# Forgetful attention: cumulative gates as a 65th row of the keys, and the first projections of one token block placed during the other block's norm

## The chip, the core and the metric

The kernel runs on one core of a Trainium2 chip. Its time is the device time of one execution in microseconds (us). Engines are named as the profile names them: PE is TensorE's matmuls and PEld its weight loads, DVE is VectorE, ACT is ScalarE, POOL is GpSimd, SP is the sync engine, which here only issues DMAs. "The granted clock" is the share of TensorE's full speed that the throttle lets through: 1.00 is 2.4 GHz and 0.50 is 1.2 GHz.

## What is computed

The kernel computes two models one after the other on 256 tokens of width 1024: a first one (a chunk mixer, a state space mixer, and two layers that gather experts from a table, "peer"), and a second one (this attention, a conv feed-forward block, a latent attention, another feed-forward block). The change touches the attention of the second model, `fox_mixer`, and the place where the first model hands over to it:

```python
def fox_mixer(h, w_in, b_f, w_out):                      # 16 heads of 64
    proj = h @ w_in                                      # queries, keys, values, 16 gate columns
    logf = log_sigmoid(proj[..., 3 * FOX_WIDTH:] + b_f)
    cum = cumsum(logf, axis=1)                           # over the 256 tokens
    ...
    sc = einsum('bqhd,bkhd->bhqk', qi, k) * scale        # per block of 128 queries
    sc = sc + (cum_q[..., :, None] - cum_k[..., None, :])
    sc = where(kpos <= qpos, sc, -inf)
    p = softmax(sc)
    return einsum('bhqk,bkhd->bqhd', p, v) ... @ w_out
```

Everything here is float32. Its input `h` is the first model's result after two RMS norms in a row (`final_g`, then `fox_norm`).

## The kernel before

Each engine has its own program, and they meet only at semaphores. `first_pe`, `first_act`, `first_dve`, `first_pool` and `first_sync` are the first model's programs, and `pe_`, `act_`, `dve_` and `sync` inside `fox` (L2586 to L2863) are the attention's. The order on an engine is the order in which the code is written.

**The hand-over.** The last part of the first model is `peer1`, which goes through expert rows: POOL gathers them, DVE takes dot products with the tokens (L1496), ACT makes weights (L1377 to L1382), and PE adds the weighted rows up (L1308). The tokens are two blocks of 128 (tb 0 and tb 1). When block 0's last sum is added to XA, `Ends` (L1526 to L1585) norms it twice (ACT L1553 squares and L1556 square roots, DVE L1575 scales), transposes it on PE (L1584), and ACT copies it to HT (L1561), all among `peer1`'s last rows. Block 1 can be normed only once `peer1` has ended: DVE L1471 and L1473 add its last sums, then the same chain runs with nothing beside it.

**The attention's start.** PE waits until both blocks are in HT. Then it forms the gate sums (L2706: the 128 tokens of a block are the weights, 16 gate columns are streamed), and `project(0, 0)`: queries and keys of two heads (L2642, all 256 tokens streamed past 128 weight columns) and values of four heads (L2651). DVE and ACT turn the gate sums into log-sigmoids LF (L2800 to L2805, with Exp and Ln on ACT).

**Pairs.** The 16 heads are done as 8 pairs, two pairs (s = 0 and 1) to a round r. For a pair PE does `scores`, then the next projection (L2642 after s = 0; L2642 and L2651 after s = 1), then `values`: six transposes of the softmax numerators (L2680) and the products with the values (L2688 to L2690). `scores` forms, for each head, a product of queries and keys over 64 rows (L2663, L2667), and adds the gates' part as a matmul too: LT is the triangle matrix times the head's column of LF, made by DVE for each pair (`gates`, L2768), and is multiplied with the matrix SUF (L2665, L2669, L2670), so that a sum over tokens between key and query comes out. Scores are formed in pieces of 128 by 128 (first query block) and 128 by 256 (second). DVE adds the causal mask (L2776), takes row maxima (L2781, L2783), ACT takes exponentials (L2733). ACT also saves what the projection left in PSUM: queries L2719, keys L2720, values L2723, and then the transposed numerators for `values` (L2740). ACT's order in a round is: exponentials, saves of the projection, copies L2740.

**Weights.** SP issues three 1 MB loads per round (L193), each into a slot that it takes when `w_used` says that the slot's last projection has ended.

After the last pair the outputs are transposed (L339) and multiplied with `fox_out` (L390).

## Time and profile before

| | us |
|---|---|
| median of 3 runs | 3567.14 (3567.11 to 3570.8) |
| the profiled execution, its own time | 3568.08 |
| its span, first to last instruction | 3566.1 |
| `peer1`'s last sums on PE end | 2701.4 |
| first scores of the attention (L2663) | 2737.9 |
| last scores of the attention end, transposes of its outputs (L339) begin | 2856.1, 2865.0 |

A row of the timeline has its start in us from the span's start, the time from the first to the last of the merged instructions, the engine, the line of the code, the operation with output and inputs, and their number; in brackets the time that the engine stood idle before it, and what ended that. One float32 matmul of the code appears in the trace as two PE instructions, each with its own weight load, so 16 matmuls are x32. Merged matmuls overlap at their ends; what counts is the distance from the start of one to the start of the next.

### The profile page before, as it was taken

The page shows a single profiled execution, that of the slowest core. Times are in us where ns is not written, and L with a number is a line of the kernel's source. Part 1 is how long each engine was busy: PE and PEld are TensorE (multiplying, and loading weights), DVE is VectorE, ACT ScalarE, POOL GpSimd, SP SyncE. Part 2 cuts the span into 40 slices and gives each one's busy share as a digit, 9 for nine tenths or more (in the row PEclk, how much of TensorE's full clock was granted, in tenths as well). Part 3 has the DMA queues.
Part 4 walks back from the last instruction along what each step waited for, and adds up shares of the span by engine and source line. Part 5 has one row for each costly group of instructions (what it writes and reads, how often), then busy time and mean ns, then how long its engine had stood idle before and what let it go on. Part 6 is the DMA issues. An engine that isn't in the chain of part 4 may idle for free.

```text
span 3566.1 us, 53144 instructions
## 1 busy us (share of the span) xinstructions
PE 2822.0 (79%) x19152; PEld 1680.4 (47%) x19152; DVE 2225.3 (62%) x5084; ACT 1393.8 (39%) x3587; POOL 854.8 (24%) x780
## 2 busy tenths in 40 slices
PE   4988898777776877786575977777767989999998
PEld 3877344233222433341144722222115879877997
DVE  5855766768777666678735467777763246523276
ACT  1213444434433334443334243334433247523275
POOL 0001433334343333433400133344440000000000
PEclk8988999999888998886677999999768999999999
DMA  8888999999999999999967699999994235433353
GB/s 328 309 313 347 419 420 420 420 420 408 421 420 394 420 414 415 413 412 387 361 224 257 256 421 421 421 414 421 416 413 159 112 124 194 156 118 109 118 192 127
DMA packets 177293, 1153.12 MB, mean 323 GB/s; under 512 B 21892, under 2 KB 30492, under 8 KB 43436
## 3 DMA queue, kind: packets, MB, share of 16 engines
q0 software_dynamic: 111632, 810.60, 55.4%
q1 hardware_dynamic: 59244, 321.94, 24.1%
q10 hardware_dynamic: 6192, 17.67, 1.3%
q8 instruction: 130, 2.13, 0.2%
q14 instruction: 95, 0.78, 0.1%
HBM read 1128.86 MB, written 21.27 MB: 323 GB/s over the span
## 4 chain that ended last, share of the span: by engine, by line
PE 40%; DMA 37%; DVE 11%; issue 6%; ACT 5%; POOL 1%; SPq 1%; ACTq 0%; DVEq 0%; POOLq 0%
DMA AR<-in_peer_uv,AR 32%; PE PS L2829 10%; PE PS L1308 6%; DVE AR L1496 4%; DMA W<-in_ada_w 3%; PE PS L1266 2%; PE PS L660 2%; PE PS L3327 2%; DVE AR L1471 2%; PE PS L2642 2%; PE PS L390 2%; PE PS L2060 2%; POOL AR L1520 1%; PE PS L521 1%; PE PS L1924 1%
## 5 line engine op out<-in xcount | busy, mean ns | idle before, releaser
L1308 PE MATMUL PS<-AR 64*64 64x512 f32 x6144 | 984.3, 720 | 498.7 <-ACT AR L1382 497.3
L1496 DVE CUSTOM_DVE_ANT_0 AR<-AR,H 128x1024 f32<-128x1024 f32 x768 | 938.4, 1224 | 540.8 <-DMA AR<-in_peer_uv,AR 534.6
L1520 POOL DMA_INDIRECT AR<-in_peer_uv,AR x768 | 850.1, 1107 | 1615.1 <-PE PS L1308 1156.8
L1308 PEld LDWEIGHTS PS<-AR 64*64 64x64 f32 x6144 | 180.1, 148 | 945.3 <-ACT AR L1382 830.0
L1377 ACT ACTIVATE SM<-SM 128x1 f32<-128x1 f32 x768 | 155.5, 202 | 1171.1 <-DVE SM L1496 1170.3
L1266 PE MATMUL PS<-HT,W 128*128 128x256 f32 x1280 | 427.8, 440 | 0.0
L1266 PEld LDWEIGHTS PS<-HT,W 128*128 128x128 f32 x1280 | 217.4, 200 | 424.7 <-issue 413.0
L1382 ACT ACTIVATE AR<-AR,SM 128x64 f32<-128x64 f32 x768 | 267.2, 348 | 25.2
L2829 PE MATMUL PS<-XP,WP 128*128 128x256 f32 x2112 | 258.4, 284 | 6.4 <-ACT AR L3003 3.5
L2829 PEld LDWEIGHTS PS<-XP,WP 128*128 128x128 f32 x2112 | 257.3, 193 | 8.7 <-DVE WP L3026 3.8
L1379 ACT ACTIVATE SM<-SM 128x1 f32<-128x1 f32 x768 | 226.3, 295 | 25.0
L660 PE MATMUL PS<-W,HT 128*128 128x256 f32 x768 | 199.4, 400 | 16.5 <-ACT AR L725 13.2
L3026 DVE TENSOR_TENSOR WP<-W,WP 128x2048 fp32r<-128x2048 f32 x62 | 141.8, 2287 | 100.3 <-ACT WP L2989 100.3
L660 PEld LDWEIGHTS PS<-W,HT 128*128 128x128 f32 x768 | 149.2, 199 | 58.9 <-issue 37.3
L1471 DVE TENSOR_TENSOR AR<-PS,AR 64x512 f32<-64x512 f32 x192 | 132.2, 689 | 5.7 <-PE PS L1308 2.2
L2829 PE MATMUL PS<-WP,GVP 128*128 128x512 f32 x528 | 129.2, 402 | 7.4 <-DVE GVP L2824 7.4
L2989 ACT CAST WP<-W 128x2048 fp32r<-128x2048 f32 x62 | 118.8, 1916 | 0.0
L2829 PEld LDWEIGHTS PS<-WP,GVP 128*128 128x128 f32 x528 | 101.5, 195 | 28.9 <-issue 8.2
L521 PE MATMUL PS<-W,SM 128*2 128x64 f32 x3072 | 65.8, 254 | 60.0 <-DMA W<-in_ada_w 56.8
L521 PEld LDWEIGHTS PS<-W,SM 128*2 128x2 f32 x3072 | 56.2, 99 | 70.7 <-DMA W<-in_ada_w 51.6
L3327 PE MATMUL PS<-HT,W 128*128 128x256 f32 x288 | 63.2, 380 | 0.8 <-ACT HT L3201 0.8
L1377 ACT ACT_TABLE_LOAD x49 | 62.9, 1283 | 0.9
(402 smaller groups left out, 3394.7 us busy)
## 6 DMA issues: line engine op xcount, KB each, us to landing
W<-in_ada_w SPq DMA_DIRECT2D x48, 1024.0 KB, 8.0
W<-in_peer_w_q SPq DMA_DIRECT2D x44, 1024.0 KB, 9.5
W<-in_ffn_out SPq DMA_DIRECT2D x22, 1024.0 KB, 4.8
W<-in_ffn_gate SPq DMA_DIRECT2D x20, 1024.0 KB, 4.8
W<-in_ffn_val SPq DMA_DIRECT2D x20, 1024.0 KB
W<-in_cm_w_in SPq DMA_DIRECT2D x16, 1024.0 KB, 8.4
AR<-min_scr SPq DMA_DIRECT2D x16, 1024.0 KB, 6.7
AR<-in_peer_uv,AR POOLq DMA_INDIRECT x768, 15.7
```

The source lines that it names most:

```text
L521: mm = pe.matmul(PS[32 * c:32 * c + 2, self.bank, j * ADA_PART:(j + 1) * ADA_PART], CS[:, k, :], W[:, s, at:at + ADA_PART], start=(k == 0) ...
L660: mm = pe.matmul(self.bank(i)[:, j * COLS:(j + 1) * COLS], HT[:, k, tb * P:(tb + 1) * P], W[:, slot, k * COLS:(k + 1) * COLS], start=(k == ...
L1266: mm = pe.matmul(PS[:, j % 2, 0:2 * P], weights[:, k * COLS + (j % 2) * P:k * COLS + (j % 2 + 1) * P], HT[:, k, first:first + 2 * P], star ...
L1308: mm = pe.matmul(PS[c * self.HP:(c + 1) * self.HP, 4 + (u % 2) * 2 + half, :], self.DIAG[rows_, r % 4, :], self.UV[rows_, r % RING, D + c ...
L1377: a.activation(self.GELU[:, u % 2, one], self.ACTV[:, u % 2, one], ACT.Gelu_apprx_tanh).then_inc(gelu_done.sem, 1)
L1379: a.mul(self.WGT[:, u % 2, one], self.GELU[:, u % 2, one], self.GATE[:, u % 2, one]).then_inc(w_ready.sem, 1)
L1382: a.mul(self.DIAG[:, r % 4, :], self.EYES, self.WGT[:, u % 2, k:k + 1]).then_inc(diag_ready.sem, 1)
L1471: one = v.tensor_tensor(self.YG[out, cols], PS[here, 4 + (u % 2) * 2 + i, :], gate[here, cols], ALU.mult)
L1496: v.tensor_tensor_reduce(rows_, rows_, H[:, self.tb(u), :], 1.0, 0.0, ALU.mult, ALU.add, self.ACTV[:, u % 2, k:k + 1]).then_inc(u_used.sem, 1)
L1520: g.indirect_dma_start(out=self.UV[:, r % RING, :], out_offset=None, in_=t["peer_uv"], in_offset=bass.IndirectOffsetOnAxis(ap=self.IDS[:, ...
L2829: mm = pe.matmul(out, lhs[i], rhs[j], start=(start and n == 0), stop=(stop and n == 2))
L3026: v.tensor_tensor(parts[:, 1, :], block_of(s, c), parts[:, 0, :], ALU.subtract).then_inc(split_done, 1)
```

## The change

- The weight columns of queries and keys are stored in another order: each 128 columns are now one head's 64 query columns and its 64 key columns, where they were 128 query columns of two heads, then their 128 key columns. A projection has the same matmuls as before. ACT's two saves take 64 partitions of 512 elements instead of 128 of 256, and keys go to KP, which now keeps all 16 heads.
- Row 65 (index 64) of KP holds minus the cumulative gates of each key, and row 65 of QP ones, so the key's part of the gates comes out of the same matmul as the product (65 rows). LT, SUF, DVE's `gates` and their matmuls go. The query's part is added by DVE with the mask, in one instruction for each piece (four in place of two).
- The cumulative gates are made once: `cumulate` does six small matmuls, ACT copies one result (16 by 256, with scale -1), SP stores it as row 65 of KP by a DMA of 16 KB, DVE copies the other result for the queries.
- Gate sums and the first projection are done token block by token block. Block 0's part (`first_rows`) is placed in PE's program before the transposes of block 1. Block 1's part stands where all of it stood.
- ACT gets a square root of one element before block 1's norms. The load of SUF goes.

```diff
@@ first_pe, first_act
             peer1.pe(ends.pe(0), lambda: drain(norm2d.pe((1,))))
+            first_chunk["fox_rows"]()
             drain(ends.pe(1))
...
             peer1.act(ends.act(0), lambda: drain(norm2d.turned((1,))))
+            a.activation(SM[:, 503:504], IDENT[:, 0:1], ACT.Sqrt)
             drain(ends.act(1))
@@ fox
-            QP, KP = view(4096, 2, SEQ), view(4608, 2, SEQ)
-            LT = view(5120, 2, SCORES)
+            QP = view(4096, 4, SEQ)
+            CUM, CI, CIJ = view(5120, SEQ), view(5376, 2, FOX_H), view(5408, 2, 2)
+            KP = view(18432, FOX_H, SEQ)
-            SUF = view(27552, 2, SEQ)
+            ONE = FOX_D + 1
@@ fox: parameters, sync
-                sp.dma_start(SUF.rearrange("p b k -> p (b k)"), t["consts"][:, C_SUF:C_SUF + 2 * SEQ]).then_inc(par_in, 16)
...
-                with sp.Fori(0, ROUNDS) as r:
+                load(0, uw[0], t["fox_qk"][0])
+                load(2, uw[2], t["fox_v"][0])
+                load(1, uw[1], t["fox_qk"][1])
+                sp.wait_ge(f_fn, 3)
+                sp.dma_start(KP[FOX_D:ONE, :, :], CUM[0:FOX_H, :]).then_inc(par_in, 16)
+                with sp.Fori(1, ROUNDS) as r:
@@ fox: new functions
+            def first_gates(tb):
+                for k in range(KT):
+                    mm = pe.matmul(PS[:, 3, tb * FOX_H:(tb + 1) * FOX_H], HT[:, k, tb * P:(tb + 1) * P], FW[:, k, :],
+                                   start=(k == 0), stop=(k == KT - 1))
+                if tb:
+                    mm.then_inc(f_sums, 1)
+
+            def first_queries(tb):
+                pe.wait_ge(w_full[0], (uw[0] + 1) * 16)
+                for i in range(2):
+                    for k in range(KT):
+                        mm = pe.matmul(PS[:, 0, i * SEQ + tb * P:i * SEQ + (tb + 1) * P], W[:, 0, k * COLS + i * P:k * COLS + (i + 1) * P],
+                                       HT[:, k, tb * P:(tb + 1) * P], start=(k == 0), stop=(k == KT - 1))
+                if tb:
+                    mm.then_inc(w_used[0], 1)
+
+            def first_values(tb):
+                pe.wait_ge(w_full[2], (uw[2] + 1) * 16)
+                for k in range(KT):
+                    mm = pe.matmul(PS[:, 2, tb * COLS:(tb + 1) * COLS], HT[:, k, tb * P:(tb + 1) * P],
+                                   W[:, 2, k * COLS:(k + 1) * COLS], start=(k == 0), stop=(k == KT - 1))
+                if tb:
+                    mm.then_inc(w_used[2], 1)
+
+            def cumulate():
+                pe.wait_ge(f_arg, 3)
+                for half, parts in enumerate((((0, 0),), ((0, P), (1, SEQ)))):
+                    for n, (tb, at) in enumerate(parts):
+                        pe.matmul(PS[0:FOX_H, 5, half * P:(half + 1) * P], LF[:, tb, :], TRI[:, at:at + P],
+                                  start=(n == 0), stop=(n == len(parts) - 1))
+                for half, parts in enumerate((((0, 0),), ((0, P), (1, SEQ)))):
+                    for n, (tb, at) in enumerate(parts):
+                        mm = pe.matmul(PS[:, 6, half * FOX_H:(half + 1) * FOX_H], TRI[:, at:at + P], LF[:, tb, :],
+                                       start=(n == 0), stop=(n == len(parts) - 1))
+                mm.then_inc(f_sums, 1)
+
+            def first_rows():
+                pe.wait_ge(n_ht.sem, ht_at - 2)
+                pe.wait_ge(par_in, 32)
+                pe.wait_ge(sums_taken.sem, st)
+                first_gates(0)
+                first_queries(0)
+                first_values(0)
@@ fox: scores
-                    pe.wait_ge(lt_ready, j * 2 + 2)
                     pe.wait_ge(s_taken, 1 + j * 2)
-                    for i, h in enumerate(heads):
-                        pe.matmul(PS[:, 3 + i, 0:P], QP[h, s, 0:P], KP[h, s, 0:P], start=True, stop=False)
-                    for i in range(2):
-                        pe.matmul(PS[:, 3 + i, 0:P], LT[:, i, 0:P], SUF[:, 0, 0:P], start=False, stop=True)
-                    for i, h in enumerate(heads):
-                        pe.matmul(PS[:, 3 + i, P:SCORES], QP[h, s, P:SEQ], KP[h, s, :], start=True, stop=False)
-                    for i in range(2):
-                        pe.matmul(PS[:, 3 + i, P:SCORES], LT[:, i, P:SEQ], SUF[:, 0, :], start=False, stop=False)
-                        mm = pe.matmul(PS[:, 3 + i, P:SCORES], LT[:, i, SEQ:SCORES], SUF[:, 1, :], start=False, stop=True)
+                    for lo, hi, keys in ((0, P, P), (P, SCORES, SEQ)):
+                        for i in range(2):
+                            mm = pe.matmul(PS[:, 3 + i, lo:hi], QP[0:ONE, 2 * s + i, lo:lo + P],
+                                           KP[0:ONE, ds(r * 4 + (2 * s + i), 1), 0:keys], start=True, stop=True)
@@ fox: start of pe_
                 pe.wait_ge(n_ht.sem, ht_at)
+                first_gates(1)
+                first_queries(1)
+                cumulate()
+                first_values(1)
                 pe.wait_ge(par_in, 48)
-                pe.wait_ge(sums_taken.sem, st)
-                for tb in range(2):
-                    for k in range(KT):
-                        mm = pe.matmul(PS[:, 7, tb * FOX_H:(tb + 1) * FOX_H], HT[:, k, tb * P:(tb + 1) * P], FW[:, k, :],
-                                       start=(k == 0), stop=(k == KT - 1))
-                mm.then_inc(f_sums, 1)
-                project(0, 0)
@@ fox: act_
-                    a.activation(QP[:, s, :], PS[:, s, 0:SEQ], ACT.Copy, scale=FOX_D ** -0.5).then_inc(qk_saved, 1)
-                    a.copy(KP[:, s, :], PS[:, s, SEQ:2 * SEQ]).then_inc(qk_saved, 1)
+                    a.activation(QP[0:FOX_D, 2 * s:2 * s + 2, :], PS[0:FOX_D, s, :].rearrange("p (h t) -> p h t", h=2),
+                                 ACT.Copy, scale=FOX_D ** -0.5).then_inc(qk_saved, 1)
+                    a.copy(KP[0:FOX_D, ds(r * 4 + 2 * s, 2), :], PS[FOX_D:P, s, :].rearrange("p (h t) -> p h t", h=2)).then_inc(qk_saved, 1)
...
-                save(0, 0)
+                save_heads(0, 0)
+                a.wait_ge(f_sums, 2)
+                a.activation(CUM[0:FOX_H, :], PS[0:FOX_H, 5, 0:SEQ], ACT.Copy, scale=-1.0).then_inc(f_fn, 1)
+                save_values(0)
@@ fox: dve_
-                def gates(j):
-                    v.wait_ge(att_sums, j)
-                    for i in range(2):
-                        for lo, hi, tb in ((0, SEQ, 0), (SEQ, SCORES, 1)):
-                            one = v.tensor_tensor(LT[:, i, lo:hi], TRI[:, lo:hi], LF[:, tb, ds(j * 2 + i, 1)].to_broadcast([P, hi - lo]), ALU.mult)
-                        one.then_inc(lt_ready, 1)
+                def query_cums(j):
+                    dve.link(v, v.tensor_copy(CIJ, CI[:, :, ds(j * 2, 2)]))
...
-                        last = v.tensor_tensor(SB[:, i, :], PS[:, 3 + i, 0:SCORES], FOX_MASK, ALU.add)
+                        for q, (lo, hi) in enumerate(PIECES):
+                            last = v.scalar_tensor_tensor(SB[:, i, lo:hi], PS[:, 3 + i, lo:hi], CIJ[:, q, i:i + 1], FOX_MASK[:, lo:hi], ALU.add, ALU.add)
...
+                dve.link(v, v.memset(QP[FOX_D:ONE, :, :], 1.0))
...
+                v.wait_ge(f_sums, 2)
+                dve.link(v, v.tensor_copy(CI, PS[:, 6, 0:2 * FOX_H].rearrange("p (t h) -> p t h", t=2)))
@@ host side: order of the weight columns (one head's 64 query columns, then its 64 key columns ...)
-        "fox_qk": blocks(np.concatenate([q, k], -1).reshape(D, -1)), "fox_v": blocks(v.reshape(D, -1)),
+        "fox_qk": blocks(np.stack([x.reshape(D, FOX_H, FOX_D) for x in (q, k)], 2).reshape(D, -1)), "fox_v": blocks(v.reshape(D, -1)),
```

On PE, at the hand-over from `peer1` to the attention, before (L1584 is the transposing of a token block, L2706 the gate sums, L2642 and L2651 the projection, L2663 the first scores; here a float32 matmul is one):

```order
L1308 MATMUL PS<-AR 64x512 x12
L1584 MATMUL PS<-CON,H 128x128 x8
L2706 MATMUL PS<-AR,HT 128x16 x16
L2642 MATMUL PS<-HT,W 128x256 x16
L2651 MATMUL PS<-W,HT 128x256 x16
```

and after (L1582 is the transposing, L2640, L2649 and L2657 are `first_gates`, `first_queries`, `first_values`, L2666 and L2670 `cumulate`):

```order
L1306 MATMUL PS<-AR 64x512 x12
L2640 MATMUL PS<-AR,HT 128x16 x8
L2649 MATMUL PS<-HT,W 128x128 x16
L2657 MATMUL PS<-W,HT 128x256 x8
L1582 MATMUL PS<-CON,H 128x128 x8
L2640 MATMUL PS<-AR,HT 128x16 x8
L2649 MATMUL PS<-HT,W 128x128 x16
L2666 MATMUL PS<-CON,AR 16x128 x3
L2670 MATMUL PS<-AR,CON 128x16 x3
L2657 MATMUL PS<-W,HT 128x256 x8
```

Half of the gate sums and of the projection now stand ahead of block 1's transposes, and the query matmuls are twice as many with half as many columns each.

On PE, the scores of a pair with the projection behind them, before:

```order
L2663 MATMUL PS<-AR 128x128 x2
L2665 MATMUL PS<-AR 128x128 x2
L2667 MATMUL PS<-AR 128x256 x2
L2669 MATMUL PS<-AR 128x256
L2670 MATMUL PS<-AR 128x256
L2669 MATMUL PS<-AR 128x256
L2670 MATMUL PS<-AR 128x256
L2637 ISA
L2639 ISA
L2642 MATMUL PS<-HT,W 128x256 x16
```

and after:

```order
L2712 ISA
L2712 MATMUL PS<-AR 128x128
L2712 ISA
L2712 MATMUL PS<-AR 128x128
L2712 MATMUL PS<-AR 128x256 x2
L2687 ISA
L2689 ISA
L2692 MATMUL PS<-HT,W 128x256 x16
```

Ten matmuls have become four, of the same shapes.

On ACT, at the same hand-over and the attention's start, before (L1553 and L1556 are the norms of block 1, L1561 the copy of its transposes):

```order
L1382 ACTIVATE AR<-AR,SM 128x64
L1553 ACTIVATE AR,SM<-XA 128x1024
L1556 ACT_TABLE_LOAD
L1556 ACTIVATE SM<-SM 128x1
L1553 ACTIVATE AR,SM<-XA 128x1024
L1556 ACTIVATE SM<-SM 128x1
L1561 COPY HT<-PS 128x4x128 x2
```

and after (two lines of the code earlier, L1551 to L1559; L2490 is the added square root):

```order
L2490 ACT_TABLE_LOAD
L2490 ACTIVATE SM<-CON 128x1
L1551 ACTIVATE AR,SM<-XA 128x1024
L1554 ACTIVATE SM<-SM 128x1
L1551 ACTIVATE AR,SM<-XA 128x1024
L1554 ACTIVATE SM<-SM 128x1
L1559 COPY HT<-PS 128x4x128 x2
```

The table load of the square root stands ahead of the first squares instead of behind them.

## Rows read from the trace of the kernel before

**Rows 1.** Windows of one core, all engines: busy us and count, granted clock, DMA.

```profile
core 0: us, PE busy (x) PEld busy (x) DVE busy (x) ACT busy (x) POOL busy (x), PEclk, DMA share, GB/s
2700.00:2722.00 22.00, 9.39 (x46) 8.11 (x46) 7.25 (x12) 6.68 (x11) 0.00 (x0) 0.61 0.37 144
2740.00:2850.00 110.00, 105.84 (x560) 90.58 (x559) 30.60 (x108) 27.33 (x87) 0.00 (x0) 1.00 0.28 104
```

**Rows 2.** TensorE's timeline: start us, us, engine, line, output<-inputs, count, idle before.

```profile
2700.29 1.09 PE L1308 MATMUL PS<-AR 64*64 64x512 f32 x8 [0.58 <-ACT AR L1382]
2713.02 1.97 PE L1584 MATMUL PS<-CON,H 128*128 128x128 f32 x8 [11.64 <-DVE H L1575]
2715.66 7.01 PE L2706 MATMUL PS<-AR,HT 128*128 128x16 f32 x32 [0.68 <-ACT HT L1561]
2722.51 8.55 PE L2642 MATMUL PS<-HT,W 128*128 128x256 f32 x32
2737.90 0.49 PE L2663 MATMUL PS<-AR 64*128 64x128 f32 x4
2738.97 0.70 PE L2667 MATMUL PS<-AR 64*128 64x256 f32 x4
2739.60 0.70 PE L2669 MATMUL PS<-AR 128*128 128x256 f32 x2
...
2741.43 7.07 PE L2642 MATMUL PS<-HT,W 128*128 128x256 f32 x32
...
2749.82 0.43 PE L2688 MATMUL PS<-AR 128*128 x2 [0.67 <-ACT AR L2740]
```

**Rows 3.** VectorE's timeline before and after the gap.

```profile
2711.68 1.29 DVE L1575 SCALAR_TENSOR_TENSOR H<-XA,SM,AR 128x1024 f32<-128x1024 f32 x1
...
2725.03 0.19 DVE L2805 SCALAR_TENSOR_TENSOR AR<-AR 128x32 f32<-128x32 f32 x1 [1.36 <-ACT AR L2754]
...
2742.09 1.02 DVE L2776 TENSOR_TENSOR AR<-PS,CON 128x384 f32<-128x384 f32 x2 [15.66 <-PE PS L2670]
```

**Rows 4.** ScalarE's timeline of the same stretch.

```profile
2706.83 1.28 ACT L1556 ACT_TABLE_LOAD   x1
...
2738.01 0.58 ACT L2723 COPY AR<-PS 128x512 f32<-128x512 f32 x1 [6.26 <-PE PS L2651]
...
2748.53 0.38 ACT L2719 ACTIVATE AR<-PS 128x256 f32<-128x256 f32 x1 [0.80 <-PE PS L2642]
2749.07 0.88 ACT L2740 COPY AR<-PS 128x384 f32<-128x384 f32 x2
```

**Rows 5.** The sync engine's timeline: issues of the first two weights.

```profile
2699.69 0.36 SPq L193 DMA_DIRECT2D W<-in_fox_qk  x1
2700.34 0.33 SPq L193 DMA_DIRECT2D W<-in_fox_v  x1
```

**Rows 6.** DMA issues: KB each, median us to landing; the first two are those of rows 5.

```profile
W<-in_fox_qk SPq DMA_DIRECT2D x1, 1024.0 KB, 4.9
W<-in_fox_v SPq DMA_DIRECT2D x1, 1024.0 KB, 6.7
AR<-in_ffn_conv SPq DMA_DIRECT2D x2, 88.0 KB, 1.9
lag_scr<-H ACTq DMA_DIRECT2D x48, 16.0 KB, 3.9
```

**Rows 7.** TensorE's timeline elsewhere: matmuls with 128 columns at the full clock.

```profile
1999.35 7.41 PE L1236 MATMUL PS<-HT,W 128*128 128x128 f32 x64 [0.73 <-ACT HT L584]
```

**Rows 8.** Windows around the gap and the end of the stage.

```profile
2716.00:2722.00 6.00, 6.00 (x30) 6.00 (x29) 0.00 (x0) 0.91 (x1) 0.00 (x0) 0.50 0.00 0
2859.00:2868.00 9.00, 7.37 (x32) 6.66 (x33) 1.04 (x5) 3.71 (x12) 0.00 (x0) 0.50 0.13 54
```

**Rows 9.** TensorE's timeline at the stage's end.

```profile
2849.58 0.82 PE L2680 MATMUL PS<-CON,AR 128*128 128x128 f32 x6
...
2859.60 1.78 PE L2680 MATMUL PS<-CON,AR 128*128 128x128 f32 x6 [3.50 <-ACT AR L2733]
```

More of the change, by code:

```diff
@@ L62 @@
 C_ALL = 1808
-C_SUF = C_ALL
 class Signal:
@@ L2632, in sync @@
                 out_sync()
+            def first_gates(tb):
[37 more added lines that the diff above has]
+                first_values(0)
+            first_chunk["fox_rows"] = first_rows
             def pe_():
@@ L2657, in scores @@
                     pe.wait_ge(qk_saved, j * 2 + 6)
-                    pe.wait_ge(lt_ready, j * 2 + 2)
                     pe.wait_ge(s_taken, 1 + j * 2)
-                    heads = [slice(i * FOX_D, (i + 1) * FOX_D) for i in range(2)]
-                    for i, h in enumerate(heads):
-                        pe.matmul(PS[:, 3 + i, 0:P], QP[h, s, 0:P], KP[h, s, 0:P], start=True, stop=False)
-                    for i in range(2):
-                        pe.matmul(PS[:, 3 + i, 0:P], LT[:, i, 0:P], SUF[:, 0, 0:P], start=False, stop=True)
-                    for i, h in enumerate(heads):
-                        pe.matmul(PS[:, 3 + i, P:SCORES], QP[h, s, P:SEQ], KP[h, s, :], start=True, stop=False)
-                    for i in range(2):
-                        pe.matmul(PS[:, 3 + i, P:SCORES], LT[:, i, P:SEQ], SUF[:, 0, :], start=False, stop=False)
-                        mm = pe.matmul(PS[:, 3 + i, P:SCORES], LT[:, i, SEQ:SCORES], SUF[:, 1, :], start=False, stop=True)
+                    for lo, hi, keys in ((0, P, P), (P, SCORES, SEQ)):
+                        for i in range(2):
+                            mm = pe.matmul(PS[:, 3 + i, lo:hi], QP[0:ONE, 2 * s + i, lo:lo + P],
+                                           KP[0:ONE, ds(r * 4 + (2 * s + i), 1), 0:keys], start=True, stop=True)
                     mm.then_inc(att_sums, 1)
@@ L2716, in act_, with save_heads, save_values @@
             def act_():
+                def save_heads(r, s):
+                    a.wait_ge(w_used[s], r + uw[s] + 2)
+                    a.activation(QP[0:FOX_D, 2 * s:2 * s + 2, :], PS[0:FOX_D, s, :].rearrange("p (h t) -> p h t", h=2),
+                                 ACT.Copy, scale=FOX_D ** -0.5).then_inc(qk_saved, 1)
+                    a.copy(KP[0:FOX_D, ds(r * 4 + 2 * s, 2), :], PS[FOX_D:P, s, :].rearrange("p (h t) -> p h t", h=2)).then_inc(qk_saved, 1)
+                def save_values(r):
+                    a.wait_ge(w_used[2], r + uw[2] + 2)
+                    a.copy(VT[:, :, ds(r * COLS, COLS)], PS[:, 2, :].rearrange("p (t c) -> p t c", t=2)).then_inc(v_saved, 1)
                 def save(r, s):
-                    a.wait_ge(w_used[s], r + uw[s] + 2)
-                    a.activation(QP[:, s, :], PS[:, s, 0:SEQ], ACT.Copy, scale=FOX_D ** -0.5).then_inc(qk_saved, 1)
-                    a.copy(KP[:, s, :], PS[:, s, SEQ:2 * SEQ]).then_inc(qk_saved, 1)
+                    save_heads(r, s)
                     if s == 0:
-                        a.wait_ge(w_used[2], r + uw[2] + 2)
-                        a.copy(VT[:, :, ds(r * COLS, COLS)], PS[:, 2, :].rearrange("p (t c) -> p t c", t=2)).then_inc(v_saved, 1)
+                        save_values(r)
                 def soft(r, s):
@@ L2784, in pair @@
                     if more:
-                        gates(j + 1)
+                        query_cums(j + 1)
                     v.wait_ge(att_exp, 1 + j * 4 + 4)
@@ L2794, in pair @@
                                             RS[:, c:c + 1], None, ALU.mult).then_inc(o_taken, 1)
-                v.wait_ge(par_in, 48)
+                dve.link(v, v.memset(QP[FOX_D:ONE, :, :], 1.0))
+                v.wait_ge(par_in, 32)
                 v.wait_ge(f_sums, 1)
-                sums = PS[:, 7, 0:2 * FOX_H].rearrange("p (t h) -> p t h", t=2)
+                sums = PS[:, 3, 0:2 * FOX_H].rearrange("p (t h) -> p t h", t=2)
                 dve.link(v, v.tensor_tensor(ZF, sums, BF.unsqueeze(1).to_broadcast([P, 2, FOX_H]), ALU.add))
@@ L2804, in dve_ @@
                 v.wait_ge(f_fn, 2)
-                dve.link(v, v.scalar_tensor_tensor(LF, ZF, 0.0, AF, ALU.min, ALU.subtract))
-                gates(0)
+                v.scalar_tensor_tensor(LF, ZF, 0.0, AF, ALU.min, ALU.subtract).then_inc(f_arg, 1)
+                v.wait_ge(f_sums, 2)
+                dve.link(v, v.tensor_copy(CI, PS[:, 6, 0:2 * FOX_H].rearrange("p (t h) -> p t h", t=2)))
+                query_cums(0)
                 with v.Fori(0, PAIRS - 1) as j:
-                    dve.enter(j, 2)
+                    dve.enter(j, 3)
                     pair(j, True)
```

4 lines of the change are left out of this document (1 added, 3 removed).

## The prediction

> **What bounds the kernel now.** I read the windows first. From 2740 to 2850, which is nearly the whole run of the eight pairs, PE is busy 105.84 of 110 us at a granted clock of 1.00, while DVE and ACT are busy 30.6 and 27.3 us and DMA has a share of 0.28 [rows 1]. So in the pairs what shortens PE's own list shortens the kernel, one to one. Ahead of them, from 2700 to 2722, PE is busy 9.39 of 22 us, at a clock of 0.61 [rows 1]. PE's timeline says why: its last `peer1` rows start at 2700.29 and end at 2701.4, then it is idle 11.64 us until DVE has normed block 1; and from 2713.02 everything that it does (transposes, gate sums 7.01 us, projection) is in line until the first scores at 2737.90 [rows 2]. That is 36.5 us from the last row of `peer1` to the first scores. The two places are independent: what is won in each adds up.
>
> **The scores (8 pairs).** Before, from the start of L2663 to the start of the next L2642: 2741.43 - 2737.90 = 3.53 us [rows 2]. After, eight PE instructions are left. Four stream 128 columns, at 7.41 / 64 = 0.116 us each by L1236 [rows 7], and four stream 256, at 7.07 / 32 = 0.221 us each by L2642 [rows 2]. That is 0.46 + 0.88 = 1.35 us, so 2.18 us less for a pair, **17.5 us for eight**. The dear side: the product over 65 rows no longer fits half of the array. The two heads' matmuls over 64 rows, whose tile is shown as 64*128, overlap: L2667's four with 256 columns take 0.63 us to the next line's start (2739.60 - 2738.97), 0.16 each, not 0.22 [rows 2]. I have already priced the new ones as full and in line. If besides each of the four matmuls exposes a weight load of about 0.12 (the price of a 128 column instruction, rows 7), a pair keeps 0.5 more, and the sum is 13.6. There is no cheaper side than full overlap, so I keep 13.6 to 17.5 and take the upper end, because L2642's row, with weights changed at each instruction, holds 0.22.
> The Trainium skill, page "TensorEngine Tiling (Array Packing)", section "The Solution" and "Theoretical Speedup", says that products over 64 rows or fewer run as two tiles at once, up to twice as fast; it speaks against a 65th row. The row above agrees, though the gain shown is 0.63 for what would be 0.88 in line, not half. By the rule alone the product would take twice its time of before, 1.26 for L2667's part and about 0.63 for L2663's with half the columns: 1.9 us a pair, 13 us saved in eight, 3546. The same page, section "Key Properties", says that a change of tiling mode drains the engine; before, a pair changes it four times, after, never.
>
> **The start.** PE's new list in its order, with the number of PE instructions in brackets.
> - Block 0's gate sums (16) begin at 2701.4. L2706 took 7.01 / 32 = 0.219 each at clock 0.50 [rows 2, 8], though it streams only 16 columns: that is the price of its weight load, and half of it, 0.11, is what I take at 1.00 (an L1236 instruction takes 0.116). To 2703.2.
> - Queries of block 0 (32) need the first weights: issued at 2699.69, landed 4.9 us later, at 2704.6 [rows 5, 6]. The clock fell in the idle stretch of before and was still at 0.50 all through 2716 to 2722, under the gate sums [rows 8], so I let it fall here too. It came back in the course of L2642, whose 32 took 8.55 in place of 7.07 us [rows 2]: 1.5 us more, that is 3.0 us at half speed. The same here: 14 instructions at 0.219 and 18 at 0.116 end at 2709.7.
> - Values of block 0 (16 at 0.22, weights landed at 2700.34 + 6.7 = 2707.0 [rows 5, 6]): 2713.2.
> - Block 1's transposes. Its rows were ready at 2713.0. The table load of 1.28 us (L1556 at 2706.83, between the squares and the first norm [rows 4]) is moved ahead of the squares into time when ACT waits for DVE, so they are ready at 2711.7. They now stand behind the new work for 1.5 us. 8 at 0.116, and 0.67 us for ACT's last copy (before, 2715.66 - 2713.02 - 1.97): 2714.8.
> - Block 1's gate sums (16) 1.8, queries (32) 3.7, `cumulate` (12, at 0.116) 1.4, values (16) 3.5: together 10.4, so 2725.2 with the clock at 1.00. Gate sums come again, so I count one more fall of the clock at the price of the first, 1.5: **2726.7**.
> So the first scores start 11.2 us earlier. Bounds: 12.7 with no second fall; and if the clock stays at 0.50 until the last values (0.219 for each 128 column instruction, 0.44 for 256), queries end at 2711.6, values at 2718.6, transposes and copy at 2721.2, the rest 3.5 + 7.0 + 2.6 + 7.0 at 2741.3: 3.4 us later than before.
> **What hides what.** The log-sigmoids are ready 2.5 us after the gate sums (2725.22 - 2722.67, rows 2 and 3), under the queries' 3.7. The new row of KP has a chain: `cumulate` ends, ACT copies (0.2 and 0.4), SP issues, the DMA lands, PE waits on it ahead of the first scores. Only values(1), 3.5 us, covers it. The nearest landings are 1.9 us (88 KB, quiet queue) and 3.9 us (16 KB, under `peer1`'s load) [rows 6]. The chain is 2.7 to 4.7, so the stall is 0 to 1.2; the queues are empty there, so I take 0. SP waits for the same copy ahead of the next round's loads; they are needed a whole pair later, so nobody notices. DVE's memset of one partition lies in the time between its norm and the gate sums, 9.7 us before (2712.97 to 2722.67, rows 3 and 2).
>
> **The saves.** ACT copies the projection 64 by 512 in place of 128 by 256: 0.58 for 512 elements (L2723), 0.38 for 256 (L2719) [rows 4], 0.2 more each, and two of them, which took 0.54 from L2719's start to L2740's. 0.4 for a pair. After s = 1 the values' projection covers this. After s = 0 nothing does: L2740 starts straight after the saves, and PE waits 0.67 us for it (L2688, rows 2). So 4 pairs lose 0.4: **1.6 us** (0 if half the partitions halve the time, 2.7, that is the 0.67 again in each, if KP's addresses cost as well).
> **The mask.** Four instructions in place of two. From L2805 (32 elements, 0.19) and L1575 (1024, 1.29) I interpolate 0.30 and 0.44 [rows 3], 1.5 us in place of 1.02. In seven pairs it is hidden: ACT was idle 0.80 us before the projection ended (2748.53, rows 4), and `gates`, which is gone, was behind the maxima anyway. In the last pair there is no projection between scores and transposes, and PE already waits 3.5 us [rows 9]: **0.3 us** lost (0 to 0.5).
> **The SUF load** is issued with `peer1`'s first weights, long before the gap, among megabytes: 0.
>
> **The sum** against the profiled execution: 3568.08 - 17.5 - 11.2 + 1.6 + 0.3 = **3541.3**. That execution lies 0.9 us above the median of the runs; I predict **3541**.
> One thing more can move the sum either way. At the stage's end PE idles 3.5 us and the clock is 0.50 from 2859 to 2868 [rows 8, 9]; the same six transposes take 1.78 and not 0.82 us there. About half of the 7.37 busy us are the price, 3.7. The idle time stays, but no row says whether the clock answers to it in the same way when it comes 27 us earlier: 4 us less or more.
>
> **Rivals.**
> - *The clock eats the start.* Two sets of gate sums, each with 16 columns, keep PE at 0.50 as L2706 did for 7 us. The scores then start between 2732 and 2741, with a middle of 2735: gain 3, time **3550**. For: rows 2 and 8. Against: under L2642, which is like the queries and values on either side, the clock came back after 3.0 us. Chance 0.16.
> - *The 65th row is dearer than its columns.* 13.6 in place of 17.5: **3545**. For: row tiles did overlap. Against: no tile changes are left. Chance 0.14.
> - *Slower.* PE's idle time behind the transposes of each s = 0 pair grows from 0.7 to 1.1 us, the scores are shorter, and so the clock, which held at 1.00 for 110 us [rows 1], starts to fall in the pairs. A fall like the one at the end lasts 9 us or more at half speed and costs about 4 us [rows 8]; twice in each of four rounds is 32 to 40 us, which gives some **3577**. It turns the sign from seven falls on. Against: the idle time stays under a tenth of a pair. Chance 0.03.
> - *The change doesn't do what it says*: PE's new rows find nothing in the gap, since block 1's transposes stand behind them and the norm ends no later. Then only the scores' gain is left, 17.5 - 1.9, and the table's 1.3: **3551**. Against: 2701.4 to 2711.7 is free for certain, and weights are there from 2704.6. Chance 0.04.
> - The forecast, **3541**, own range 3536 to 3546: 0.63.
>
> Range 3535 to 3551. A difference of 0.2% is 7 us, about what a measurement of this kernel can tell from no change; only the slower rival and its partial forms (two to six falls) end above 3560. Faster 0.95, same 0.03, slower 0.02.
>
> **What would show it.** In the profile after: a pair's scores take 1.35 us from their start to the next projection; PE's idle time of 11.64 us is gone but for about 1.3 us before the first queries; block 1's transposes start near 2713.2 on a busy PE; first scores near 2727; no wait on the DMA of 16 KB longer than 1 us; PE waits for L2740's successor 1.1 us in s = 0 pairs; a granted clock of 1.00 through the pairs. It is wrong if scores take over 1.9 us, if they start after 2731, or if the clock in the pairs is under 0.95.

## The result and the profile after

| | before | after |
|---|---|---|
| median, first timing | 3570.8 (5 runs) | 3553.59 (3543.21 to 3559.13, 5 runs) |
| ratio, three timings, with 95% interval | | 0.9945 [0.9933, 0.9957], 0.9921 [0.9905, 0.9936], 0.9942 [0.9926, 0.9958] |
| profiled execution, its own time | 3568.08 | 3558.82 |

The change makes the kernel faster: the medians of the first timing lie 17.2 us apart, and the ratios of the three timings say 0.55 to 0.79%, which is 20 to 28 us (a ratio is not the quotient of the two medians; the first one's would be 0.9952). The prediction was 3541 and its range ended at 3551: the direction was right, the time lies outside. Single executions of the changed kernel scatter over 16 us (3543.2 to 3559.1).

TensorE's timeline of the kernel after, from `peer1`'s last row to the first scores and the projection behind them (columns as in rows 2):

```profile
2709.59 1.09 PE L1306 MATMUL PS<-AR 64*64 64x512 f32 x8 [1.39 <-ACT AR L1380]
2710.61 1.96 PE L2640 MATMUL PS<-AR,HT 128*128 128x16 f32 x16
2713.35 6.72 PE L2649 MATMUL PS<-HT,W 128*128 128x128 f32 x32 [0.78 <-DMA W<-in_fox_qk]
2719.91 3.62 PE L2657 MATMUL PS<-W,HT 128*128 128x256 f32 x16
2723.36 1.04 PE L1582 MATMUL PS<-CON,H 128*128 128x128 f32 x8
2725.12 1.96 PE L2640 MATMUL PS<-AR,HT 128*128 128x16 f32 x16 [0.72 <-ACT HT L1559]
2726.93 3.82 PE L2649 MATMUL PS<-HT,W 128*128 128x128 f32 x32
2730.68 0.83 PE L2666 MATMUL PS<-CON,AR 128*16 128x128 f32 x6
2731.44 0.84 PE L2670 MATMUL PS<-AR,CON 128*128 128x16 f32 x6
2732.13 3.70 PE L2657 MATMUL PS<-W,HT 128*128 128x256 f32 x16
2735.67 1.48 PE L2712 MATMUL PS<-AR 65*128 x8
2736.98 7.07 PE L2692 MATMUL PS<-HT,W 128*128 128x256 f32 x32
```

The 11.64 us of idle time [rows 2] are gone; two short waits are left, 0.78 for the first weights and 0.72 for ACT's copy. A pair's scores take 2736.98 - 2735.67 = 1.31 us where they took 3.53 (1.36 to 1.37 in the later pairs, whose scores in turn start 0.22 us behind the last product with the values, where it was 0.31). But `peer1`'s last row starts at 2709.59, 9.3 us later than before, although the code ahead of it is the same.

Windows of the same kernel: the pairs from 2736, and three stretches in and behind them (columns as in rows 1):

```profile
2736.00:2846.00 110.00, 101.05 (x509) 87.72 (x507) 28.92 (x111) 33.04 (x91) 0.00 (x0) 0.94 0.36 135
2777.50:2784.20 6.70, 6.70 (x19) 5.36 (x18) 3.64 (x14) 1.47 (x7) 0.00 (x0) 0.50 0.08 34
2811.60:2815.00 3.40, 3.40 (x10) 2.69 (x9) 2.83 (x10) 0.04 (x1) 0.00 (x0) 0.50 1.03 436
2842.40:2862.70 20.30, 14.73 (x51) 11.69 (x50) 7.37 (x19) 10.15 (x18) 0.00 (x0) 0.50 0.32 134
```

The granted clock in the pairs is 0.94, where 1.00 was shown [rows 1]: it falls twice inside them, and at the stage's end it stays at 0.50 for 20 us, where it was 10 in the profile of before. What a fall costs is seen in the two pairs in which the falls inside lie, and what PE waits for in the pairs, in its timeline (L2712 begins a pair):

```profile
2743.89 0.82 PE L2723 MATMUL PS<-CON,AR 128*128 128x128 f32 x6
2745.94 0.43 PE L2731 MATMUL PS<-AR 128*128 x2 [1.24 <-ACT AR L2787]
...
2747.32 1.53 PE L2712 MATMUL PS<-AR 65*128 x8
2748.69 7.07 PE L2692 MATMUL PS<-HT,W 128*128 128x256 f32 x32
2755.60 7.07 PE L2701 MATMUL PS<-W,HT 128*128 128x256 f32 x32
...
2765.42 1.53 PE L2712 MATMUL PS<-AR 65*128 x8
...
2777.13 2.58 PE L2712 MATMUL PS<-AR 65*128 x8
2779.50 9.43 PE L2692 MATMUL PS<-HT,W 128*128 128x256 f32 x32
2788.77 7.07 PE L2701 MATMUL PS<-W,HT 128*128 128x256 f32 x32
...
2798.58 1.53 PE L2712 MATMUL PS<-AR 65*128 x8
...
2810.30 1.64 PE L2712 MATMUL PS<-AR 65*128 x8
...
2830.07 1.53 PE L2712 MATMUL PS<-AR 65*128 65x128 f32 x8
...
2847.97 1.78 PE L2723 MATMUL PS<-CON,AR 128*128 128x128 f32 x6 [3.87 <-ACT AR L2780]
```

The scores and the projection of queries and keys take 2.37 and 9.27 us from start to start in the pair of the first fall, and 1.37 and 6.91 in the pair from 2747.32. The whole pairs say the same: 18.09 us without a fall (2765.42 - 2747.32), 21.45 with the one of 6.8 us (from 2777.13), 19.77 with the one of 3.4 us (from 2810.30). A fall costs half its length, 3.4 and 1.7 us. Behind the transposes PE waits 1.24 us (0.67 in rows 2), and ahead of the last transposes 3.87 (3.50 in rows 9). ScalarE's timeline of the kernel after shows the longer wait's cause, and that the square root's table is loaded early:

```profile
2709.56 1.28 ACT L2490 ACT_TABLE_LOAD   x1
...
2732.32 0.37 ACT L2804 ACTIVATE AR<-PS 16x256 f32<-16x256 f32 x1 [0.33 <-PE PS L2670]
...
2744.09 0.59 ACT L2759 ACTIVATE AR<-PS 64x512 f32<-64x512 f32 x1 [0.77 <-PE PS L2692]
2744.70 0.58 ACT L2761 COPY AR<-PS 64x512 f32 x1
2745.31 0.86 ACT L2787 COPY AR<-PS 128x384 f32<-128x384 f32 x2
```

The two saves take 2745.31 - 2744.09 = 1.22 us, where they took 0.54 [rows 4]: each is longer, and they no longer overlap (0.61 us apart at a duration of 0.59, where before the second started 0.29 us behind the first at 0.38). The cumulative gates' row arrives in time; of the DMA issues this one has 16 KB and lands in 2.1 us, and PE goes on from L2657 to L2712 without a wait:

```profile
AR<-AR SPq DMA_DIRECT2D x1, 16.0 KB, 2.1
```

### The profile page after: what moved, and what is told of

Same layout as the page of the kernel before. It is cut to its first block, busy times and chain, and to the rows that moved or that the text cites. A ratio compares the mean times of both kernels' runs of the same rounds, so it can differ in the third digit from the quotient of the medians.

```text
span 3556.7 us, 53022 instructions
## 1 busy us (share of the span) xinstructions
PE 2810.8 (79%) x19100; PEld 1680.0 (47%) x19100; DVE 2221.2 (62%) x5078; ACT 1398.8 (39%) x3589; POOL 861.2 (24%) x780
## 4 chain that ended last, share of the span: by engine, by line
PE 41%; DMA 36%; DVE 10%; issue 6%; ACT 5%; POOL 1%; SPq 1%; ACTq 0%; DVEq 0%; POOLq 0%
DMA AR<-in_peer_uv,AR 31%; PE PS L2878 10%; PE PS L1306 6%; DVE AR L1494 4%; DMA W<-in_ada_w 3%; PE PS L658 3%; PE PS L1264 3%; PE PS L3376 2%; PE PS L388 2%; PE PS L2058 2%; DVE AR L1469 2%; PE PS L2692 1%; POOL AR L1518 1%; PE PS L519 1%; PE PS L1922 1%
## 5 line engine op out<-in xcount | busy, mean ns | idle before, releaser
L658 PE MATMUL PS<-W,HT 128*128 128x256 f32 x768 | 207.1, 411 | 15.7 <-ACT AR L723 13.9
```

The costliest lines, as they stand in the source:

```text
L658: mm = pe.matmul(self.bank(i)[:, j * COLS:(j + 1) * COLS], HT[:, k, tb * P:(tb + 1) * P], W[:, slot, k * COLS:(k + 1) * COLS], start=(k == ...
```

## The experiments

Every kernel's profile is cut at the same three points: the start of the last PE instruction of `peer1`, the first scores, and the first transpose of the attention's outputs (where "pairs" ends). "0.50 in pairs" is the time at half clock between the last two of them, with what lies at the stage's end.

| kernel | up to `peer1`'s last | start | pairs | 0.50 in pairs | rest | median (runs), ratio to before |
|---|---|---|---|---|---|---|
| before, profile 1 | 2700.8 | 37.1 | 127.1 | 6.5 | 701.1 | |
| before_again | 2703.3 | 37.9 | 127.1 | 5.7 | 705.2 | 3575.8 (1) |
| after, profile 1 | 2710.1 | 25.6 | 117.7 | 21.3 | 703.4 | 3553.6 (5), 0.9945 |
| after_again | 2714.2 | 25.0 | 118.6 | 19.5 | 701.7 | 3551.8 (6), 0.9921 |
| after_third | 2702.1 | 25.2 | 114.8 | 15.4 | 699.8 | 3559.4 (6), 0.9942 |
| after_wide | 2709.5 | 25.2 | 115.2 | 12.6 | 705.2 | 3555.4 (4), 0.9938 |
| scores_only | 2706.1 | 37.4 | 117.2 | 20.4 | 700.8 | 3571.9 (12), 0.9977 |
| start_only | 2711.7 | 24.1 | 127.1 | 5.7 | 705.3 | 3564.7 (6), 0.9958 |
| turned_first | 2700.0 | 25.4 | 110.7 | 11.1 | 703.3 | 3543.1 (5), 0.9927 |
| fill | 2704.8 | 25.5 | 110.2 | 0.0 | 700.4 | 3539.9 (5), 0.9913 |
| fill_turned | 2699.3 | 25.0 | 107.5 | 0.0 | 699.2 | 3535.8 (5), 0.9903 |
| fill_turned_again | 2711.0 | 25.7 | 107.5 | 0.0 | 699.8 | 3544.8 (6), 0.9907 |
| start_fill | 2705.0 | 23.6 | 107.5 | 0.0 | 700.1 | 3539.6 (4), 0.9911 |
| no_preload | 2707.9 | 25.0 | 107.5 | 0.0 | 699.1 | 3541.4 (1) |

Medians were taken on five occasions, and those of before ranged from 3569.9 to 3579.6, so kernels are compared by ratio or by their own stretches. The 95% intervals of the ratios are 0.0012 to 0.0022 to either side. after_again, after_wide, scores_only and start_only were timed together, and so were fill, turned_first and fill_turned.

**after_again and before_again** are the two kernels unaltered.

> The changed kernel, not altered, for a second profile and five more times. Theory 1 (the granted clock falls at other moments in each execution): the time up to the last row of peer1, which was 2710.1 us in the first profile of the changed kernel and 2700.8 before, differs again by several us, anywhere between 2698 and 2712, and the stretch from there to the transposes of the attention's outputs, 143.3 us in the first profile, lies between 139 and 147 according to the number of clock falls in it. The five times spread over 10 us or more, with a median near 3552. Rival (something in the change makes all that stands ahead of the attention slower): peer1's last row is at 2710 again, within 1.5 us, and so in every variant of the changed kernel.

> The kernel before, not altered, for a second profile. Theory 1 (the time up to peer1's last row differs from execution to execution, and the profile on which the prediction rested was a short one): that row is between 2706 and 2715, as in the five profiles since, and not at 2700.8; the start takes 37.1 us and the pairs 127.1 again, within 1 us. Rival (all the changed kernels are slower there): it is at 2700.8 again, within 2 us.

Measured: 2714.2 and 2703.3. The first lies 2.2 us above what theory 1 gave; the rest of that expectation came true (143.6 us from there to the outputs' transposes, a median of 3551.8). The second lies below what theory 1 gave and half a microsecond outside what the rival gave, so before_again alone decides nothing. Together with the others it does: the changed code reached that point between 2699.3 and 2714.2, on either side of before's 2700.8 and 2703.3, and start_only, which has before's pairs, at 2711.7. The rival's "within 1.5 us of 2710" is wrong. The last rows of `peer1` on PE, of before_again and of after_third:

```profile
2702.83 1.09 PE L1308 MATMUL PS<-AR 64*64 64x512 f32 x8 [1.39 <-ACT AR L1382]
```

```profile
2701.59 1.09 PE L1306 MATMUL PS<-AR 64*64 64x512 f32 x8 [1.39 <-ACT AR L1380]
```

**after_wide** keeps the wide table and its load:

```diff
+C_SUF = C_ALL
...
+                sp.dma_start(view(27552, 2, SEQ).rearrange("p b k -> p (b k)"), t["consts"][:, C_SUF:C_SUF + 2 * SEQ]).then_inc(par_in, 16)
...
-    c = np.zeros((P, C_ALL), np.float32)
+    c = np.zeros((P, C_SUF + 2 * SEQ), np.float32)
```

> The changed kernel with the wide table of constants and the load of its last 512 columns kept as before, although nothing reads them; all that is issued and laid out ahead of the gap is then as in the kernel before, up to the attention's own PE, ACT and DVE code. Rival (the narrower table or the missing load makes the first 2700 us slower by 9): peer1's last row is back near 2700.8 and the median falls to about 3543. Theory 1 (clock): no shift that differs from other executions; median 3552, within 5 us of the changed kernel.

Measured: 2709.5 and a ratio of 0.9938. Neither the table nor the load explains the 9.3 us.

**scores_only** keeps the change on the scores and puts block 0's part back behind block 1's transposes:

```diff
-            first_chunk["fox_rows"]()
...
-            a.activation(SM[:, 503:504], IDENT[:, 0:1], ACT.Sqrt)
...
                 pe.wait_ge(n_ht.sem, ht_at)
+                first_rows()
                 first_gates(1)
```

> The changed kernel with block 0's gate sums, queries and values moved back behind block 1's transposes, and without the added square root: only the part on the scores and the cumulative gates is left of the change. By the prediction's sum it keeps 17.5 less 1.9 of saves and mask; by the first profile of the changed kernel a pair's scores take 1.31 us (2.2 less), the saves cost 0.54 more in each of 4 pairs, and clock falls in the pairs cost 5, so 8 to 15 us faster than before: ratio 0.996 to 0.998. Rival (clock falls in the pairs come from the start being earlier, not from the pairs): no fall inside the pairs, 15 us faster.

**start_only** is the kernel before with `first_gates`, `first_queries`, `first_values` and `first_rows` as in the change (without `cumulate`), the call, and the square root:

```diff
                 pe.wait_ge(n_ht.sem, ht_at)
+                first_gates(1)
+                first_queries(1)
+                first_values(1)
                 pe.wait_ge(par_in, 48)
...
-                project(0, 0)
```

> The kernel before with only the start changed: block 0's gate sums and projection ahead of block 1's transposes, and the square root ahead of block 1's norms; scores, LT and SUF as before. From peer1's last row to the first scores 37.1 us before, 25.6 in the changed kernel less 1.6 for the cumulative sums: 24 here, so 13 us faster, ratio 0.9963. If the clock falls in the pairs come from the changed pairs (more idle time behind the transposes, shorter scores), there is none here and from first scores to the transposes of the outputs it takes 127 us as before; the rival, that they come from the phase of the execution alone, lets them appear here too (130 or more).

Measured: the two halves add up, 0.23% and 0.42% to 0.65%. The start alone takes 24.1 us, 13.0 less, with the pairs at 127.1 and no clock fall in them but the one at the stage's end. The scores alone take the pairs to 117.2, with falls at the same kind of place though the start is the old one; the gain of 0.23%, 8 us, is at the small end of what was expected. Two windows of scores_only and one of start_only:

```profile
2785.70:2789.10 3.40, 3.40 (x10) 2.69 (x9) 2.24 (x9) 0.00 (x0) 0.00 (x0) 0.50 0.08 31
2816.40:2823.20 6.80, 6.80 (x20) 5.63 (x20) 3.69 (x14) 0.84 (x4) 0.00 (x0) 0.50 0.87 367
```

```profile
2736.00:2855.00 119.00, 113.32 (x606) 96.05 (x606) 32.39 (x114) 29.06 (x91) 0.00 (x0) 1.00 0.33 120
```

So the falls come from the changed pairs. In the four profiles of the changed kernel (after_wide among them) there are nine inside the pairs: 2, 4, 1 and 2. Each begins 0.3 to 1.4 us after the start of a pair's scores, right behind the values of the pair ahead: four behind an s = 0 pair, where PE's wait grew, and five behind an s = 1 pair, where it is 0.71 us as before. One of the latter, in after_again:

```profile
2767.57 0.43 PE L2731 MATMUL PS<-AR 128*128 x2 [0.71 <-ACT AR L2787]
...
2768.95 1.87 PE L2712 MATMUL PS<-AR 65*128 x8
```

```profile
2770.00:2773.30 3.30, 3.30 (x10) 2.59 (x9) 2.43 (x9) 0.00 (x0) 0.00 (x0) 0.50 0.13 52
```

**fill** (and **fill_turned**, with 2 in place of 4) gives PE work whose result nobody reads:

```diff
+                def fill(n):
+                    for _ in range(n):
+                        pe.matmul(PS[:, 7, 384:512], IDENT, IDENT, start=True, stop=True)
...
+                    if last:
+                        pe.wait_ge(o_taken, 1 + j * 4)
+                        fill(14)
...
                     pe.wait_ge(o_taken, 1 + j * 4)
+                    fill(2 if s else 4)
```

> The changed kernel with matmuls of the unit matrix, whose result nobody reads, where PE would wait: 4 (about 0.9 us) behind the transposes of each s = 0 pair, 2 (0.5 us) behind those of each s = 1 pair, 14 (3.3 us) between the last pair's scores and its transposes. Theory 2 (the clock falls in the pairs because PE's list has lost dense work and gained idle time): no fall between the first scores and the transposes of the outputs, that stretch takes 112 us or less in place of 115.2 to 118.6, and the kernel is 4 to 8 us faster than the changed one. Rival (the falls have nothing to do with the idle time): two or more falls as before, and no gain or a loss of 1 us.

**turned_first** (and fill_turned) changes ACT's order:

```diff
                         soft(r, s)
-                        if s == 0:
-                            save(r, 1)
-                        elif more:
+                        if s == 1 and more:
                             save(r + 1, 0)
                         save_turned(r, s)
+                        if s == 0:
+                            save(r, 1)
```

> The changed kernel with ACT's order changed in s = 0 pairs: the copies of the transposes (which PE waits for) come first, the saves of the projection behind them. Theory 3 (the longer saves, 0.6 each in place of 0.27, stand between PE and its values): PE's wait for those copies falls from 1.24 to about 0.5 us in the four s = 0 pairs, a new wait of 0.1 to 0.7 for the saves comes ahead of the next scores, and 1 to 3 us are won. If shorter single waits keep the clock up as well, there are fewer falls in the pairs than the two to four of the changed kernel. Rival: the wait only moves to the scores, 0 us.

> Both: the copies first, and 2 unit matmuls (0.5 us) behind the transposes of every pair, 14 in the last. Theory 2 and 3 together: no fall in the pairs, 110 us from the first scores to the transposes of the outputs, 6 to 10 us faster than the changed kernel. Rival: not different from fill.

Measured: with fill there is no fall at all from the first scores to the outputs' transposes, and the pairs take 110.2 us. With turned_first one short fall is left in the pairs beside the one at the end, and they take 110.7. With both, 107.5. The windows of the pairs in fill, PE's timeline of a pair in turned_first, and the window of the fall that turned_first has left:

```profile
2731.00:2840.00 109.00, 105.64 (x600) 94.29 (x598) 30.41 (x118) 35.31 (x101) 0.00 (x0) 1.00 0.39 145
```

```profile
2733.60 0.82 PE L2723 MATMUL PS<-CON,AR 128*128 128x128 f32 x6
2734.76 0.43 PE L2731 MATMUL PS<-AR 128*128 x2 [0.34 <-ACT AR L2787]
```

```profile
2767.00:2770.30 3.30, 3.30 (x10) 2.54 (x9) 2.83 (x10) 0.20 (x1) 0.00 (x0) 0.50 0.03 10
```

fill adds work to PE and takes none from any engine; all that the profile shows on the other side is the clock. No profile with unit products (five of them) has a fall in the pairs, and every one of the changed pairs without them (six) has at least one. By time fill is 3 to 11 us faster than the changed kernel, if ratios from different chips are set side by side (0.9913 against 0.9921 to 0.9945); 4 to 8 was expected.

In turned_first the wait behind the transposes went from 1.24 to 0.34 us, and an s = 0 pair takes 0.7 us less (11.0 for 11.7), so 2.8 us in four: that lies within the expected 1 to 3. The rest of its gain is that it has one fall of 3.4 us where four profiles of the changed kernel have one to four; whether the order makes them fewer, one profile can't tell, and its ratio (0.9927) is not clear of theirs. But that fall says something: every wait of PE behind the transposes is 0.34 or 0.71 us there, none longer than before the change (0.67 and 0.72), and the clock fell all the same. So a longer wait isn't needed for a fall; what is left that differs in PE's list is the shorter scores. That rests on one fall in one profile, against none in three profiles with the old pairs. fill_turned is 2.7 us shorter in the pairs than fill; by time the two can't be told apart.

**after_third and fill_turned_again** put the two on one chip.

> The changed kernel once more, on the same chip as fill_turned_again, so that the two can be set side by side. Start 25.0 to 25.6, pairs 115 to 119 with two to four clock falls; the time up to peer1's last row anywhere from 2699 to 2714; median 3548 to 3556.

> fill_turned once more beside it. By the profiles the pairs take 107.5 in place of 115 to 119, so the median is 8 to 12 us below the changed kernel's; if the earlier 15 us between their medians on different chips came from the pairs alone it would be the same again here, and if from chance in the first 2700 us, less.

Measured: 3559.44 and 3544.83, 14.6 apart, with intervals of the ratios that only touch (0.9942 [0.9926, 0.9958], 0.9907 [0.9889, 0.9926]). Their pairs differ by 7 to 11 us; the rest is scatter of the other stretches or not explained. after_third's median lies 3.4 us above what was expected, and the difference of the two above the expected 8 to 12.

**start_fill and no_preload.** start_fill is fill_turned with unit products in the start too, at two places (`fill3` writes PS[:, 3, 384:512]):

```diff
                 first_gates(0)
+                fill3(4)
                 first_queries(0)
...
+                fill3(3)
                 pe.wait_ge(n_ht.sem, ht_at)
```

> fill_turned with unit matmuls at the start too: 4 (0.9 us) between block 0's gate sums and its queries, where PE waits 0.8 us for the first weights, and 3 (0.7 us) between block 1's transposes and its gate sums, where it waits 0.7 us for ACT's copy. In all profiles of the changed start the clock was at 0.50 for 6.8 us, during block 0's queries. If the idle time there brings that on, the start takes 22 to 23 us in place of 25.0 to 25.6; rival (the gate sums with their 16 columns and peer1's last rows bring it on): 25 again, within 0.5.

> fill_turned without the added square root, for a look at the start alone. The prediction had block 1's rows ready ahead of PE, so the table load of 1.28 us, back between the squares and the first norm, should be hidden behind block 0's queries and values: the start takes 25.0 to 25.6 as with it. Rival (the load is part of the chain): 1.28 us more.

Measured: start_fill's start has no time at 0.50 and takes 23.6 us, 1.5 less, less than expected: block 0's queries and values are now done before block 1 is normed. The queries of block 0 in the kernel after (6.72 us, above) and in start_fill, with the transposes' new wait:

```profile
2708.31 3.74 PE L2649 MATMUL PS<-HT,W 128*128 128x128 f32 x32
...
2716.22 1.09 PE L1582 MATMUL PS<-CON,H 128*128 128x128 f32 x8 [0.40 <-DVE H L1573]
```

no_preload is fill_turned without its square root:

```diff
-            a.activation(SM[:, 503:504], IDENT[:, 0:1], ACT.Sqrt)
```

Its start takes 25.0 us, as fill_turned's does: the table load was hidden.

The fastest kernel of the study is fill_turned, 0.9903 [0.989, 0.9917] and 0.9907 [0.9889, 0.9926] of before; start_fill, with 1.5 us less by the profile, can't be told from it by time.

## Why the prediction was wrong

Forecast and profile of the kernel after differ by 3558.8 - 3541.3 = 17.5 us, and the three points share this out: 9.3 ahead of the attention, -0.3 in the start, +6.2 in the pairs, +2.3 behind. Only the middle two belong to what the change does.

- **The basis.** The sum started from one profiled execution and took all that the change leaves alone as fixed. It isn't: in 14 profiles `peer1`'s last row comes between 2699.3 and 2714.2, and the mean is 2706.1. The profile of before was among the earliest. The clock's time at 0.50 up to there was 703 to 782 us in these profiles, 710 in that of before, but it does not order them (fill has 775 and 2704.8), so what makes the scatter is not settled. The stretch behind the attention scatters too, from 699.1 to 705.3. Within the ratios this evens out: 12.3 us from the start and 10.5 from the pairs (means of the three profiles of after and one of after_wide, against the two of before) are 22.8 us, 0.64%; measured were 0.55, 0.79 and 0.58%. The forecast gain was 26.8 us. So of the 12.3 us between the forecast and the first median, 4.0 are the change's own, 2.7 are that the kernel before had a median of 3570.8 there and not 3568.1, and 5.6 are that this timing showed 17.2 of the 22.8 us.
- **Scores.** 1.35 us forecast, 1.31 to 1.37 measured; with the 0.09 us by which seven of them start sooner, 18.0 us gained where 17.5 were forecast. The eight instructions run in line at full pace, so the rival of a dearer 65th row is wrong, and so are the 1.9 us a pair that the prediction worked out for dearer products over 65 rows.
- **The start.** 25.9 us forecast (37.1 - 11.2), 25.0 to 25.6 measured. The pieces are close but for the clock: it was at 0.50 once for 6.8 us, under block 0's queries, which take 6.56 us where block 1's take 3.75, and not at all under block 1's. One fall at 2.8 us in place of two at 1.5: that this sum came out is luck. The table load was shown as a gain in the argument and counted for nothing in the sum, and no_preload bears that out. The rival in which the clock stays down was wrong, and so was that in which the gap is not used.
- **The saves.** 0.4 us a pair forecast, 0.57 measured (1.24 - 0.67), because the two no longer overlap: 2.3 us in place of 1.6. The mask: 0.37 for 0.3, by PE's wait ahead of the last transposes.
- **The step that failed: the clock in the pairs.** With the scores, the saves and the mask as measured the pairs should take 127.1 - 18.0 + 2.3 + 0.4 = 111.8, and so do the pairs without a fall if they are added up (three of 18.09, four of 11.66 to 11.71, a last one of 10.78). They took 114.8 to 118.6, 116.5 in the mean: 5.0 us over the forecast's 111.5. The forecast wrote "a granted clock of 1.00 through the pairs", and its rival of falls in the pairs stood at 0.03 as a whole, with the partial forms only named, and those wrongly placed: it has two to six falls end above 3560, but at its own 4 us each two falls give 3549, and only five or more pass 3560. A fall inside the pairs in the forecast's own case had no price, and it is what happens: 12.6 to 21.3 us at half speed, against 5.7 to 6.5 before. The rival's mechanism (idle time beside shorter scores) is the right one in the main; its size was wrong both ways, with one to four falls in place of eight, and 1.7 or 3.4 us in place of 4 for one. The Trainium skill, page "TensorE: Matmul & The Clock Gate", section "A second HAM failure mode: psum-queue depth-cycling", tells of a kernel whose short idle times between groups of matmuls let the clock go down and up again; the trace after agrees, with 0.94 and waits of 0.7 and 1.24 us, and this rule should have been weighed against the saves' 0.4 us. fill shows that the falls go when PE's idle time in the changed pairs is filled. That idle time grew from 0.67 to 1.24 us in s = 0 pairs, and 2.2 us of scores beside it had gone; turned_first, which has a fall with no wait longer than before, speaks for the second as enough by itself; how many of the falls the first adds is open. The upper end of the range, 3551, was set by the start alone, and neither the scatter of the basis nor the falls stood in it.

## What to carry to other kernels

Here part of the gain from work removed beside PE's waits was paid back by the clock, 0.94 where it had been 1.00, though no single wait inside the pairs was longer than 1.24 us. So where TensorE bounds a stage, count what idle time stands next to what is removed, and try filling it or moving the wait before the gain is booked. A reorder of another engine's list (what the bound engine waits for first, what it needs later second) won 0.7 us in each of four pairs with no work removed. And before a change of half a percent is forecast from one profile, ask for a second of the same kernel: 15 us of scatter in code that nobody touched is as large as the effect.

## What was not expected of the hardware

ACT's two saves of 64 partitions by 512 elements each start 0.61 us apart at a duration of 0.59, so they don't overlap; the two of 128 by 256 that they replace started 0.29 us apart at 0.38 [rows 4], whose second row is:

```profile
2748.82 0.37 ACT L2720 COPY AR<-PS 128x256 f32<-128x256 f32 x1
```

The Trainium skill, page "ScalarE: Activation LUTs", section "What ACT_TABLE_LOAD costs", says that activations in a row overlap by about 93 ns: the old pair agrees with 0.09, the new pair does not.

Matmuls whose result nobody reads made the stage shorter. In fill there are 38 (4 in each of four pairs, 2 in each of the other four, 14 more in the last), of two PE instructions each, which is 76 x 0.116 = 8.8 us of PE's time. The granted clock in the pairs went from 0.94 to 1.00 with them, and the stage from 114.8 to 118.6 us down to 110.2. That is 1.6 us below the 111.8 of pairs without a fall inside: 1.2 of these are in the last pair (9.6 for 10.8 us), where unit products stand in the wait of 3.87 us and the clock no longer falls (before the change it fell there as well).
